# Sample tile in quarters of the TensorE array, first late modulation chunks requested during its head norms, last routing tile in halves of the model width

## The reference, cut to what matters

```python
mod = silu(c) @ w_ada + b_ada                        # six rows of 1024: shift, scale, gate, twice
h = modulate(rmsnorm(x, g_mix), sh_a, sc_a)
u = h @ w_in                                         # 1024 -> 2208: q, k, v (512 each), q_lat 384, kv_lat 256, kpe 32
q_sb = rmsnorm(q heads, g_sb_q); k_sb_new = rmsnorm(k heads, g_sb_k)
qm = rmsnorm(q_lat, g_qa) @ w_qb                     # 8 heads of 64 + 32
q_mla = [rmsnorm(qm nope), rope(rmsnorm(qm pe))]
ckv_new = rmsnorm(kv_lat, g_kva); kpe_new = rope(rmsnorm(kpe_raw))
kv = ckv_all @ w_kvb; k_nope = rmsnorm(kv nope)      # sample: cached latents and new ones
x = x + gt_a * (concat(stick-breaking attention, softmax attention) @ w_out)
h2 = modulate(rmsnorm(x, g_ffn), sh_m, sc_m)
x = x + gt_m * (top-1 group of 4, top-2 of its 8 experts, expert width 256)(h2)
```

## Time and profile before

| | us |
|---|---|
| runs before, median (lowest to highest) | 1363.47 (1362.73 to 1366.17) |
| the profiled execution: its own time | 1369.1 |
| its span | 1367.1 |
| busy in the span: PE / DVE / ACT / POOL | 1232.2 / 692.2 / 372.1 / 215.3 |
| DMA queue of SP, share of 16 engines | 39.1% |

### The profile page before, as it was taken

The page is one execution under the profiler, slowest core; times in us unless marked ns, Lnnn a source line. Parts: engine busy times, 40 slices in busy tenths (PEclk is TensorE's granted clock), DMA queues, the critical chain, the costliest instruction groups (busy, mean ns, idle before and its releaser), DMA issues. The chain is left out here.

```text
span 1367.1 us, 17659 instructions
## 1 busy us (share of the span) xinstructions
PE 1232.2 (90%) x6498; PEld 700.4 (51%) x6499; DVE 692.2 (51%) x1316; ACT 372.1 (27%) x826; POOL 215.3 (16%) x249
## 2 busy tenths in 40 slices
PE   4999999999959978989999999899929999989885
PEld 1555555555415556656666666455524444444441
DVE  1245543445546866466666673455533444444342
ACT  1122222222223443455454543233320000000000
POOL 0000000000000001433333231011131222222222
PEclk9999999999958999799999999899959999999997
DMA  8712111111038852221100004452249999999962
GB/s 364 273 46 62 37 56 62 47 46 51 22 97 299 305 210 63 82 54 29 28 10 20 1 1 156 162 185 93 77 167 407 329 382 380 359 346 355 340 209 34
DMA packets 94158, 213.41 MB, mean 156 GB/s; under 512 B 22097, under 2 KB 56003, under 8 KB 78722
## 3 DMA queue, kind: packets, MB, share of 16 engines
q1 hardware_dynamic: 85858, 195.05, 39.1%
q0 software_dynamic: 8224, 17.34, 5.1%
HBM read 186.60 MB, written 35.71 MB: 163 GB/s over the span
## 5 line engine op out<-in xcount | busy, mean ns | idle before, releaser
L2086 PE MATMUL g_GU<-w_gu,g_xT 128*128 128x512 f32 (+1 forms) x432 | 163.8, 598 | 2.1 <-DVE g_xT L2291 1.4
L1710 PE MATMUL f_C<-first_region,oT 128*128 128x512 f32 x256 | 116.3, 608 | 0.0
L419 PE MATMUL U<-w_in_sb,b_hT 128*128 128x512 f32 x256 | 112.3, 593 | 0.0
L2086 PEld LDWEIGHTS g_GU<-w_gu,g_xT 128*128 128x128 f32 (+1 forms) x432 | 64.2, 172 | 81.0 <-issue 80.4
L2101 PE MATMUL g_Y<-w_down,g_hT 128*128 128x512 f32 (+1 forms) x216 | 87.7, 618 | 0.5 <-issue 0.5
L1523 DVE TENSOR_TENSOR_SCAN e_stick<-e_stick 128x128 f32<-128x128 f32 (+7 forms) x64 | 86.6, 1374 | 0.2 <-POOL e_stick L1332 0.2
L419 PE MATMUL b_UL<-w_in_sb,b_hT 128*128 128x384 f32 (+2 forms) x272 | 79.3, 451 | 3.4 <-DMA w_in_sb<-w_in 3.4
L2295 DVE TENSOR_TENSOR g_sig<-g_GU,g_sig 128x256 f32<-128x256 f32 x26 | 11.0, 424 | 133.0 <-ACT g_sig L2263 133.0
L1710 PEld LDWEIGHTS f_C<-first_region,oT 128*128 128x128 f32 x256 | 48.5, 195 | 54.9 <-issue 54.8
L419 PEld LDWEIGHTS U<-w_in_sb,b_hT 128*128 128x128 f32 x256 | 47.6, 190 | 54.1 <-issue 54.0
L1389 PE MATMUL e_Z<-first_region,work 96*128 96x512 f32 (+3 forms) x192 | 75.2, 520 | 0.0
(11 more groups left out here) (387 smaller groups left out, 2172.4 us busy)
## 6 DMA issues: line engine op xcount, KB each, us to landing
w_gu<-w_gate SPq DMA_DIRECT2D x27, 1024.0 KB, 12.1
w_gu<-w_up SPq DMA_DIRECT2D x27, 1024.0 KB, 25.6
w_down<-w_down SPq DMA_DIRECT2D x27, 1024.0 KB, 24.2
key_region<-w_ada SPq DMA_DIRECT2D x16, 1024.0 KB, 5.1
w_in_sb<-w_in SPq DMA_DIRECT2D x3, 2048.0 KB, 17.3
first_region<-w_gate SPq DMA_DIRECT2D x5, 1024.0 KB, 12.6
first_region<-w_up SPq DMA_DIRECT2D x5, 1024.0 KB, 22.2
first_region<-w_down SPq DMA_DIRECT2D x5, 1024.0 KB, 19.4
```

Of the source, the lines that this page charges most:

```text
L419: end = nc.tensor.matmul(dst[0:T, 0:c1 - c0], lhsT=hT[:, k, 0:T], rhs=g.w_in[:, k, c0:c1], start=k == 0, stop=k == KD - 1)
L1710: end = nc.tensor.matmul(C[n % 2][:, c * 512:(c + 1) * 512], lhsT=g.oT[:, k, i * P:(i + 1) * P], rhs=wo[:, k, c * 512:(c + 1) * 512], star ...
L2086: end = nc.tensor.matmul(GU[h * n:h * n + n, :], lhsT=xT[:, k, h * n:h * n + n], rhs=wgu[s][:, :, k, :], start=k == 0, stop=k == KD - 1, t ...
```

## The change

1. **Sample tile in quarters** (`sample()` on PE, ACT, DVE and SP in place of `body(PT)` and the last two `back`). Each of q and k is cut in four pairs of heads; pair j of q and pair j of k go side by side into column group j of one PSUM bank (`U[0]`, 4 x 256 columns). A second set of four holds query latents (384), two halves of v (256 each) and key latents (256). kpe is projected by the full array on `hT` written four times over. `w_qb` and `w_kvb` (its key half alone; the values of the sample's new latents are not made any more, nothing reads them) are cut in four too. Head norms then work on 128 partitions x 256, 192 or 128 columns. The turned latents go to other banks than the last prompt tile's transposes, and its `back` parts lie between.
2. **Late chunks.** The first two chunks of `w_ada` for block CD are requested in `sample()` of SP, right after the sample tile's projections; `key_region` is now a view of the memory of `w_in`, as are most buffers of blocks CD and E.
3. **Last routing tile in halves** (n = `END` = 8): residual, square, `h2`, transpose, copy and logits in two halves of 512 columns with semaphores of their own; the exponentials of tile 7 come behind the copy of tile 8's `h2T`, and the last two fetches of the square-root table are left out.

```diff
+def load_late(nc, io, g, sp, t):
+    b, half, k = t % 2, t // KD, t % KD
+    sp.dma_start(g.key_region[:, b * 2 * D:(b + 1) * 2 * D],
+                 io["w_ada"][k * P:(k + 1) * P, (half + 1) * 2 * D:(half + 2) * 2 * D]).then_inc(g.wa_in[b], 16)
...
+        PAIR = 2 * SBD
+        qk4 = qk[:].rearrange("p h d -> p (h d)")[:, 0:2 * PAIR]
```

SyncE in block B:

```diff
+            def sample():
+                sp.wait_ge(side_mm, 1)
+                for t in range(2):
+                    load_late(nc, io, g, sp, t)
+                sp.wait_ge(kpe_done, NT)
...
+                queries_out(PT - 1)
+                sp.wait_ge(qk_norm, NT)
+                for j in range(SBH // 2):
+                    sp.dma_start(io["o_k_s"][:, j * PAIR:(j + 1) * PAIR], qk4[j * DEC:(j + 1) * DEC, PAIR:]
+                                 ).then_inc(st_k, 16)
```

TensorE in block B:

```diff
+            def sample():
...
+                for k in range(KD):
+                    flags = dict(start=k == 0, stop=k == KD - 1)
+                    qk_cols = g.w_in[:, k, 0:2 * SBW].rearrange("p (a n) -> p a n", a=2)
+                    for j in range(4):
+                        nc.tensor.matmul(U[0][j * DEC:(j + 1) * DEC, 0:2 * PAIR], lhsT=hT[:, k, 0:DEC],
+                                         rhs=qk_cols[:, :, j * PAIR:(j + 1) * PAIR], tile_position=(0, j * DEC), **flags)
+                    for j, (dst, c0, w) in enumerate(beside):
+                        nc.tensor.matmul(dst[j * DEC:(j + 1) * DEC, 0:w], lhsT=hT[:, k, 0:DEC],
+                                         rhs=g.w_in[:, k, c0:c0 + w], tile_position=(0, j * DEC), **flags)
+                for k in range(KD):
+                    end = nc.tensor.matmul(UL[:, 1, 0:ROPE], lhsT=hT[:, k, :], rhs=g.w_in[:, k, INC - ROPE:],
+                                           start=k == 0, stop=k == KD - 1)
+                end.then_inc(side_mm, 1)
+                back(PT - 1, 0)
+                pe.wait_ge(lat_norm, NT)
...
+                back(PT - 1, 1)
+                pe.wait_ge(latTa_done, NT)
+                for k in range(QR // P):
+                    for j in range(4):
+                        nc.tensor.matmul(UL[j * DEC:(j + 1) * DEC, 0, 0:2 * MK], lhsT=qlatT[:, k, 0:DEC],
+                                         rhs=g.w_qb[:, k, j * 2 * MK:(j + 1) * 2 * MK], start=k == 0,
+                                         stop=k == QR // P - 1, tile_position=(0, j * DEC))
```

SyncE in block CD (`body(t)`, the load now under `if later(t, 1)`):

```diff
-                half, k = t // KD, t % KD
-                sp.dma_start(wa[:, b], io["w_ada"][k * P:(k + 1) * P, (half + 1) * COLS:(half + 2) * COLS]
-                             ).then_inc(wa_in[b], 16)
+                    load_late(nc, io, g, sp, t)
```

ScalarE in block FR, and the shared memory:

```diff
+            def norm_halves(n):
+                b = n % 2
+                act.wait_ge(x2_half, 1)
...
+                nc.scalar.activation(half_st[:, 1:2], half_st[:, 0:1], ACT.Identity, bias=g.eps[:]).then_inc(sq_half, 1)
+                act.wait_ge(x2_done, n + 1)
...
+                nc.scalar.activation(st[:, b, 1:2], st[:, b, 0:1], ACT.Sqrt, bias=half_st[:, 1:2]).then_inc(rms, 1)
...
-                nc.scalar.activation(st[0:1, 0, 3:4], g.eps[0:1], ACT.Sqrt)
+                if n < END - 1:
+                    nc.scalar.activation(st[0:1, 0, 3:4], g.eps[0:1], ACT.Sqrt)
...
-                if n < NT:
+                if n < END:
                     norm(n)
-                if n:
+                elif n == END:
+                    norm_halves(n)
+                else:
+                    exponents(END - 1)
+                if n and n != END:
                     exponents(n - 1)
...
+            g.region = m.sb("region", [P, KD * INC])
+            g.key_region = g.region[:, 0:SBH // 2 * SEQ]
```

More of the change, by code:

```diff
@@ L352, in queries_out @@
                              ksT[:, :, 0:T]).then_inc(st_ks, 16)
-                sp.wait_ge(e3, i + 1)
+                if not last(i):
+                    sp.wait_ge(e3, i + 1)
                 sp.wait_ge(e2, i + 1)
@@ L385, in _ @@
             tiles(sp, body)
+            sample()
             for t in range(2):
@@ L467, in body @@
                     pe.wait_ge(in_q, 16)
-                if not last(i):
-                    project(U[0], 0, SBW, T, q_mm)
+                project(U[0], 0, SBW, T, q_mm)
                 if not first:
@@ L518, in _ @@
             tiles(pe, body)
-            back(PT, 0)
-            back(PT, 1)
+            sample()
         @block.scalar
@@ L612, in _ @@
             tiles(act, body)
-            back(PT)
+            sample()
         @block.vector
@@ L700, in body @@
                 end.then_inc(qk_norm, 1)
-                if not last(i):
-                    xn_of(i + 1)
-                    hT_of(i + 1)
+                xn_of(i + 1)
+                hT_of(i + 1)
                 dve.wait_ge(qm_evac, i + 1)
@@ L1882, in residual @@
                 b = n % 2
+                if n == END:
+                    dve.wait_ge(st_x2[b], 16 * (n // 2))
+                    dve.wait_ge(x_in[b], 16 * (n // 2) + 16)
+                    for sem, value, done, cols in ((pr_half, 1, x2_half, HALVES[0]), (pr_mm, n + 1, x2_done, HALVES[1])):
+                        dve.wait_ge(sem, value)
+                        step(V.tensor_tensor(x2[:, b, cols], C[b][:, cols], rows[:, 0, 0, cols], ALU.mult))
+                        V.tensor_tensor(x2[:, b, cols], x2[:, b, cols], xr[:, b, cols], ALU.add).then_inc(done, 1)
+                    return
                 dve.wait_ge(pr_mm, n + 1)
@@ L1903, in normed @@
                     dve.wait_ge(st_h2, 16 * n)
+                if n == END:
+                    for done, cols in ((h2_half, HALVES[0]), (h2_done, HALVES[1])):
+                        step(V.scalar_tensor_tensor(h2[:, cols], x2[:, b, cols], st[:, b, 2:3], rows[:, 1, 0, cols],
+                                                    ALU.mult, ALU.mult))
+                        V.tensor_tensor(h2[:, cols], h2[:, cols], rows[:, 2, 0, cols], ALU.add).then_inc(done, 1)
+                    return
                 step(V.scalar_tensor_tensor(h2[0:T], x2[0:T, b], st[0:T, b, 2:3], rows[0:T, 1, side, :],
```

369 lines of the change are left out of this document (269 added, 100 removed).

## The result

The changed kernel takes 1346.29 us (median of 4 runs, 1343.91 to 1351.78) beside 1364.26 of the kernel before: a ratio of 0.9873, interval 0.9838 to 0.9909. With six more runs it was 1347.11 us and 0.9879 (0.9854 to 0.9904), so it gains 16.5 us by the ratio, from 13 to 20 (15.4 us by the two medians of that comparison). The forecast was 25.3 us and 1338.2; the time lies just above its range, which ended at 1346.

The account below looks back on a forecast made before the run. TensorE, busy 90% of the span, was taken as the bound, with time to win only where it idles or runs at half clock. Gains of 15.0 + 5.0 + 5.3 = 25.3 us gave 1338.2 us, range 1331 to 1346.

Parts of the forecast that it names:

- the list of costs at nothing: Costs counted as zero: new positions in memory and eight wider `hT` writes, 0.1 us each; without cover 0.8 us.
- a later block gives part back: Rival, 6%: block G runs at the transfers' limit, so another order of transfers could cost 10 us: 1348.
- (a): Sample tile's projections in four column groups: end at 371.0 instead of 369.8, 1.2 us lost.
- The rule weighed there: Tiling-mode changes drain TensorE, at most 0.16 us each; four more would take 0.6 us off the gain; nothing was added.
- (b): Sample tile, projections to heads' end: `w_qb` and `w_kvb` leave the path; TensorE ends near 377.9, last copy at 378.7.
- the named lower end: Sample tile: if the clock is halved already at 374, the gain is 2.5 us less.
- (c): Sample tile's MLA head norms, 11.1 us before: now from 378.7 to 383.1.
- (d): Last norm to block CD: the 4.4 us stay, SyncE is free at 383.2, block CD starts at 387.4.
- the rival of 3%: Projections, 3%: column groups run one by one and their weight loads show; 18 us slower, 1381.
- The constant between profile and median: Whole kernel: median of runs taken as 5.6 us below the profiled execution, so 1343.8 becomes 1338.2.
- the marks set beforehand: Signs, including block CD near 387, no `c_S` wait; wrong if CD after 391, projections after 374, E or G over 2 us changed.

Follow-up runs that it names:

- the queries first: Changed kernel with idle-time transposes in the sample tile, 156 met waits, and SyncE's query and key stores ahead of the cache loads: 1341.0 us, ratio 0.9840.
- part 1 alone: Kernel before with only the sample tile in quarters: 1357.3 us, ratio 0.9952.
- the run of parts 1 and 3: Changed kernel with the first two chunks of `w_ada` again requested in block CD: 1352.6 us, ratio 0.9919.
- the busy sample tile: Changed kernel with 25 unused transposes of the identity on TensorE while it waits for the last head norms and block CD: 1347.5 us, ratio 0.9896.

## Why the prediction was wrong

- **Part 1 carries the whole error.** Forecast 15.0 us, 6.5 in the medians. Ahead of block CD 4 us are missing: it starts at 390.1 to 391.5 in the kernels with this part (389.0 with the queries first), beside 401.3 to 402.7. Behind block CD's start some 4.5 are missing.
- **The step that failed most was the list of costs at nothing.** The sum counted the additional records of the projections (144 for 80) for their time on TensorE and on no other account. With their weight loads they move TensorE's instruction stream by half a load, and a stop that fell nowhere now falls at the end of block CD. Moving the stream by another half load takes 4.4 us from the changed kernel and 4.9 from part 1 alone, and adds 5.5 to the kernel before. The stops seen in the traces are about 2 us of that; how the rest hangs on the place of the stream is not shown. The rival "a later block gives part back" had the form of it, but named block G and its transfers; block G kept its length.
- **(a) Projections**: end at 371.88, forecast 371.0. 0.6 us of that is the start, 361.18 here and 360.55 in the first profile of before (361.62 in the second); from start to end they took 10.7 us, forecast 10.4. The rule weighed there, that a change of tiling mode drains TensorE (the Trainium skill, "TensorEngine Tiling (Array Packing)", section Key Properties), would have given 371.6. In the rows the group's records of 384 columns follow each other by 0.32 us; behind the last two, from 369.17 on, the next would start at 369.81, and the first full-array record starts at 369.91. So 0.10 us at this change, where the bound was 0.16 and the sum had 0. Four changes at that price would be 0.4 us, an estimate that the 0.3 us left do not contradict; the change of mode was not tried alone.
- **(b) To the heads' end**: key and value heads of the sample were there at 380.7, forecast 377.9. The clock had halved before `w_qb`, which took 1.76 us where the forecast had 1.0, after four of tile 7's transposes had gone from 0.60 to 1.06. This was the named lower end, and it came in this profile. But block CD starts no earlier where it did not come (the heads 7.2 us behind the projections in the run of parts 1 and 3, 8.8 in the second profile of the changed kernel, and block CD 18.7 and 18.8 behind them), so it cost less than it seems.
- **(c) Head norms**: from the start of the squares (381.25) to the last norm (385.56) 4.3 us, forecast 4.4. Right, but 2.5 late by (b).
- **(d) To block CD**: forecast "SyncE [...] is free at 383.2, just in time". It was free at 385.17, 2.0 us later, and then waited 0.6 us for the norms; in the runs whose norms came earlier it was SyncE that held the block. The term mis-sized is "twelve or so issues of 0.43 us from 376 on": it was fourteen, from 377.07 on, and the four pieces of `o_k_s` among them cost 0.72 each. The 4.4 us from the last norm to the block's start were 4.6 in this profile (385.56 to 390.12), and 6.6 with the busy sample tile.
- **Part 2**: forecast 5.0, measured 6.2 to 6.5 at the third turn (11.06 behind the block's start, 17.26 and 17.57 before) and 5.4 in the medians. Right, and so is its step: the second key product starts 7.7 us behind the block's start (forecast 7.8) and takes 1.96 us (1.88). The chunks landed in time, and neither the queries nor `c_pc` nor the first latents were waited for.
- **Part 3**: forecast 5.3, measured 4.9 at block G's start and 4.6 in the medians. Right; the logits at half clock took 3.48 us, forecast 3.6.
- **The quarters do not take turns** (the rival of 3%): the projections end 2 us later than before, not 20.
- **The constant between profile and median** (5.6 us) was sound in the main: 4.4 us of it are block E at a granted clock of 0.96 instead of 0.99. But that the first pair of profiles differs by 24.8 us, so near the forecast of 25.3, is luck: more runs and a second profile of each kernel were needed to see that the gain is 16.5.
- Of the marks set beforehand, no wait of `c_S` and projections by 374 held, and block CD started at 390.1 and 391.5, on both sides of the mark of 391; "blocks E or G change their length by over 2 us" was too fine a mark, since block E scatters by 5 us without any change.

## What to carry to other kernels

Additional instructions on an engine can cost more than their time, or give time back, by moving everything behind them against the borders of the instruction loads: look at the instruction queue's loads in the DMA view, and at "issue" rows in dense stretches of short records anywhere behind the change. If a gain at a block's start does not arrive at the end, compare starts block by block over two profiles of each kernel, and run the parts alone. And when several chains end within a microsecond or two, cost the DMA issues of the last one by their own rows, not by a mean.

## What the runs showed of the hardware

- Instructions arrive in loads of 16 KB, 48 on TensorE's queue in 1342 us; in a product of 128 records at 15.5 ns each it stopped 1.2 to 1.5 us at a load's border, and up to 3.2 us where the border lies in a product some 50 instructions earlier in the stream. Half a load of idle instructions at the start of the program moved the median of three kernels by 4.4 to 5.5 us, up in one and down in two.
- 256 waits that are already met are 128 instructions of TensorE's queue. They delayed the first products by 4.5 us in the changed kernel (13.23 to 17.75), and 0.6 us of that was left at the first product of block B (34.04 to 34.67), which waits for its weights in either case.
- Work without use did not keep the clock through a wait: in the run with the busy sample tile TensorE stood 4.7 us ahead of block CD, and the block's first product took 3.78 us, as at half clock, though the 11 transposes ahead of the wait had run at full.
